# Two-layer retention, Fourier and convolution backbone on one core: stacked retention states, norm roots by column groups, low halves on GpSimd, other orders in the mixers and in the first output stage

## The chip, the cores and the metric

One NeuronCore of a Trainium2 chip runs the whole program. The metric is the device time of one execution in microseconds (us). The engines are named as the profile names them: PE (TensorE matmul), PEld (its weight loads), DVE (VectorE), ACT (ScalarE), POOL (GpSimd), SP (SyncE, which issues most DMAs; SPq is its queue). L1251 is line 1251 of the kernel before.

## The reference

Two layers over a latent stream x (512 tokens of 1024 channels) and a context stream (256 tokens), all float32. Cut to what matters here:

```python
for l in range(2):
    sh1, sc1, g1, sh2, sc2, g2 = split(silu(c) @ w_mod[l] + b_mod[l])          # six modulation vectors, per stream
    h = rmsnorm(x) * (1 + sc1) + sh1                                          # context likewise
    q, k, v, gate, f, cb, cc, ch = split(h @ w_in[l])                         # 3072 columns
    o  = retention(rope(q), rope(k), v) forwards + the same backwards         # 8 heads of 64, chunks of 128 tokens
    o  = o * rsqrt(mean(o * o, per head) + eps) * silu(gate)
    y  = concat(o, real(fft2(f)), cb * dwconv3(cc * ch))
    x  = x + g1 * (y @ w_out[l])
    h  = rmsnorm(x) * (1 + sc2) + sh2
    val, g = split(dwconv3(h @ w_up[l], w_conv))
    x  = x + g2 * ((val * silu(g)) @ w_down[l])
return rmsnorm(x) * final_norm_g
```

Retention of a chunk is the masked scores times the values (intra), plus the queries, scaled by a per-row decay xi, times the state before the chunk (cross). The state of a direction is `S <- decay * S + k^T (zeta * v)`, a 64x64 matrix per head. The latent scans start from the states that the two context chunks leave.

## The kernel before

**Dense products.** Activations lie transposed, channels on partitions. Each weight matrix is cut into "slabs" of 128 output channels by 1024 inputs (512 KB). SP loads them one after the other from HBM (`load_slab`, L328), together with the modulation weights (`load_mods`, L342), which VectorE reduces against the conditioning vectors with a custom dot product (L737) and finishes at L740. GpSimd splits every slab in two halves of four blocks, each into a rounded high part `w_hi` (L446) and a low part `w_lo` (L448), and counts four `split` per slab. TensorE makes one 128x128 block of a slab (a "tile", L1251) from three products in the fast float32 format, hi·hi, lo·hi and hi·lo: six matmuls for both streams in layer 0 (512 latent and 256 context columns), three in layer 1, where the context only feeds kv. Two pairs of PSUM banks alternate between slabs.

**Norms.** The n1_0 norm at the start sums the squares with matmuls whose weights are 128 columns of squares and whose moving operand is a column of ones (L1340), so that one column of results comes for each 128 tokens; ScalarE takes the square roots, VectorE the reciprocals, and TensorE spreads them over the partitions with the identity (L1439). The other norms (n2_0, n1_1, n2_1) come in two parts, one for each stream or half, with sums at L1375 and roots at L1384. For each of eight channel blocks of a part VectorE scales (L877), ScalarE adds the shift and rounds to `h_hi` (L545), VectorE takes the rest `h_lo` (L883), and `part_tile` (L1359) uses both at once.

**The mixer.** After the kv and q slabs, `mixer_plan` (L138) deals the steps of retention evenly among the 96 tiles of the cch, cbf and g slabs (conv, Fourier and gate columns); all engines walk through this one list. A state step is 8 matmuls (L1539) for one direction and one chunk; VectorE makes `vz` (L1037) just before and adds into the state just after (L1047 to L1052). The states of a head pair lie as two 64x64 blocks in a 128x128 block that is zero elsewhere; memsets clear them (L941). A chunk is four steps: scores (L1555), out (cross product of both directions L1569, intra L1575), sums of squares per head (L1583, 4 matmuls with two moving columns) and roots spread per head (L1590, 8 matmuls). On VectorE these are qxi (L1065), the masked scores St (L1069), the reciprocal (L1073) and the product (L1077). Layer 0 has 10 state steps and 6 chunks, layer 1 10 and 4. TensorE waits for all transposed keys (`k_moved`) before the list begins; the last rope (L956 to L958, Y block 3) comes on VectorE at the first chunk's scores. After the list come the channel transforms of the Fourier part (L1606 to L1612) and its sequence products (L1640, L1644), then the out stage.

**Other pieces.** ScalarE makes the decay tables (L475 to L484) and VectorE combines them (`log_decays` L760 to L772, `decays` L779 to L784), in layer 0 right after the first norm and the first kv slab. In the out stage of layer 0 SP brings two slabs and six pairs of mods for the second norm in an order written out by hand. `keep_busy` issues matmuls of no use to anyone while TensorE would wait.

## Time and profile before

| | us |
|---|---|
| median of 3 executions | 1621.41 |
| lowest, highest | 1615.40, 1622.27 |
| the profiled execution's own time | 1619.17 |
| its span in the profile | 1617.4 |
| busy in the span: PE, DVE, POOL, ACT | 1559.5, 919.3, 888.8, 331.7 |
| share of PE and of DVE in the chain that ended last | 64%, 22% |
| HBM read | 165.44 MB, 104 GB/s over the span |
| mean granted clock of TensorE | 0.983 of full speed |

The busy time of an engine is a sum over its instructions. Matmuls overlap in the pipeline, so the time of a group of them is best read from the start of its first to the start of what comes next.

### The profile page before, as it was taken

What the parts mean: (1) busy time and instruction counts of PE and PEld (TensorE: products, weight loads), DVE (VectorE), ACT (ScalarE), POOL (GpSimd) and SP (SyncE); (2) the same over time, 40 slices, a digit from 0 to 9 for tenths busy, and PEclk for the clock granted to TensorE, in tenths of its full rate; (3) what the DMA queues carried; (4) which work ended last, traced back from release to release, by engine and by line L of the source; (5) the groups of instructions that cost most, each with busy time, mean ns of one, the idle gap of its engine ahead of it and who ended that gap; (6) DMA issues with size and microseconds to landing.
All of it is one profiled execution on the core that took longest, in us unless ns stands there. A gap on an engine that the chain in (4) does not pass through costs nothing.

```text
span 1617.4 us, 24334 instructions
## 1 busy us (share of the span) xinstructions
PE 1559.5 (96%) x8962; PEld 1325.4 (82%) x8962; DVE 919.3 (57%) x1367; ACT 331.7 (21%) x512; POOL 888.8 (55%) x830
## 2 busy tenths in 40 slices
PE   7989999999999999999999999999998999999997
PEld 5778888887788888888888888877778888888886
DVE  3876444498887865873378646454545441341444
ACT  3602111311312101120021224111223220220221
POOL 2264333475455565654565544554464776777764
PEclk7999999999999999999999999999999999999999
DMA  8453111244234343332333323231222323233223
GB/s 333 146 168 100 58 40 40 89 154 145 92 130 130 110 142 115 128 130 77 106 125 109 105 80 100 82 92 53 66 78 66 104 93 100 92 99 108 91 91 105
DMA packets 50082, 172.63 MB, mean 107 GB/s; under 512 B 6241, under 2 KB 8801, under 8 KB 48993
## 3 DMA queue, kind: packets, MB, share of 16 engines
q1 hardware_dynamic: 46080, 165.70, 30.6%
q10 hardware_dynamic: 3936, 6.06, 1.3%
q8 instruction: 42, 0.69, 0.2%
q14 instruction: 24, 0.19, 0.0%
HBM read 165.44 MB, written 2.10 MB: 104 GB/s over the span
## 4 chain that ended last, share of the span: by engine, by line
PE 64%; DVE 22%; issue 7%; ACT 3%; DMA 2%; POOL 1%; DVEq 1%; ACTq 1%; SPq 0%
PE pair L1251 51%; DVE aux L737 6%; PE pair L1359 5%; DVE tg L1189 3%; DVE tv L1189 3%; DVE hid_lo L1217 1%; DVE tv L1214 1%; ACT tv L707 1%; ACT hid_hi L715 1%; PE aux L1569 1%; DMA raw<-in_slabs 1%; PE aux L1539 1%; PE aux L1640 1%; DVE h_lo L883 1%; DVE mod_acc L737 1%
## 5 line engine op out<-in xcount | busy, mean ns | idle before, releaser
L446 POOL TENSOR_SCALAR w_hi<-raw 128x512 fp32r<-128x512 f32 (+1 forms) x412 | 298.5, 725 | 674.3 <-PE pair L1251 530.7
L448 POOL TENSOR_TENSOR w_lo<-raw,w_hi 128x512 fp32r<-128x512 f32 (+1 forms) x412 | 592.0, 1437 | 34.4
L1251 PE MATMUL pair<-h_hi,w_hi 128*128 128x512 f32 x1760 | 530.7, 359 | 13.9 <-DVE tv L1189 5.0
L1251 PE MATMUL pair<-h_lo,w_hi 128*128 128x512 f32 x1760 | 523.5, 355 | 1.6 <-DVE h_lo L1091 1.4
L1251 PE MATMUL pair<-h_hi,w_lo 128*128 128x512 f32 x1760 | 521.7, 354 | 0.0
L1251 PEld LDWEIGHTS pair<-h_hi,w_hi 128*128 128x128 f32 x1760 | 288.6, 189 | 66.5 <-issue 13.1
L1251 PEld LDWEIGHTS pair<-h_lo,w_hi 128*128 128x128 f32 x1760 | 288.8, 189 | 51.1 <-DVE h_lo L1091 3.1
L1251 PEld LDWEIGHTS pair<-h_hi,w_lo 128*128 128x128 f32 x1760 | 288.6, 189 | 45.9
L737 DVE CUSTOM_DVE_ANT_0 aux<-mod_slot,c_b 128x1024 f32<-128x1024 f32 x160 | 234.8, 1467 | 4.8 <-DMA mod_slot<-in_mods 2.1
L1144 DVE SCALAR_TENSOR_TENSOR x<-pair,modv,x 128x256 f32 (+3 forms) x84 | 53.0, 658 | 169.0 <-PE pair L1251 168.8
L1251 PE MATMUL pair<-hid_hi,w_hi 128*128 128x512 f32 x486 | 146.8, 356 | 0.2 <-POOL w_lo L448 0.2
L1251 PE MATMUL pair<-hid_lo,w_hi 128*128 128x512 f32 x486 | 146.9, 356 | 0.1
L1251 PE MATMUL pair<-hid_hi,w_lo 128*128 128x512 f32 x486 | 146.7, 356 | 0.0
L1189 DVE SCALAR_TENSOR_TENSOR tg<-pair,vecs,tg 128x511 f32<-128x511 f32 (+1 forms) x132 | 87.0, 659 | 83.2 <-ACT tg L710 75.1
L1189 DVE SCALAR_TENSOR_TENSOR tv<-pair,vecs,tv 128x511 f32<-128x511 f32 (+1 forms) x132 | 87.2, 661 | 81.0 <-ACT tv L707 72.7
L1251 PEld LDWEIGHTS pair<-hid_lo,w_hi 128*128 128x128 f32 x486 | 80.1, 188 | 14.5 <-DVE hid_lo L1217 0.8
L1251 PEld LDWEIGHTS pair<-hid_hi,w_hi 128*128 128x128 f32 x486 | 80.1, 188 | 14.3 <-issue 0.5
L1251 PEld LDWEIGHTS pair<-hid_hi,w_lo 128*128 128x128 f32 x486 | 80.2, 188 | 13.8
L707 ACT ACTIVATE tv<-pair,vecs 128x768 f32<-128x768 f32 (+1 forms) x44 | 35.0, 796 | 260.1 <-PE pair L1251 205.9
L710 ACT ACTIVATE tg<-pair,vecs 128x768 f32<-128x768 f32 (+1 forms) x44 | 35.1, 798 | 178.6 <-PE pair L1251 178.5
L1217 DVE TENSOR_TENSOR hid_lo<-tv,hid_hi 128x768 f32 (+1 forms) x44 | 43.1, 980 | 44.7 <-ACT hid_hi L715 44.7
L713 ACT ACTIVATE tg<-tg 128x768 f32<-128x768 f32 (+1 forms) x44 | 32.6, 741 | 137.4 <-DVE tg L1189 137.4
(177 smaller groups left out, 1329.6 us busy)
## 6 DMA issues: line engine op xcount, KB each, us to landing
raw<-in_slabs SPq DMA_DIRECT2D x206, 512.0 KB, 3.5
mod_slot<-in_mods SPq DMA_DIRECT2D x80, 512.0 KB, 3.5
start_slot<-in_start_mods SPq DMA_DIRECT2D x8, 1024.0 KB, 15.4
x<-in_x SPq DMA_DIRECT2D x4, 768.0 KB, 9.6
rot<-kT ACTq DMA_DIRECT2D x32, 64.0 KB, 2.0
rot<-Y ACTq DMA_DIRECT2D x32, 64.0 KB, 2.1
out<-fin SPq DMA_DIRECT2D x16, 128.0 KB, 1.9
c_b<-in_c SPq DMA_DIRECT2D x1, 512.0 KB, 7.6
```

What stands on the lines that cost most here:

```text
L446: nc.gpsimd.tensor_scalar(w_hi[p][:, a:b], raw[p][:, a:b], 1.0, 1.0, ALU.mult, ALU.mult).then_inc(split, 1)
L448: nc.gpsimd.tensor_tensor(w_lo[p][:, a:b], raw[p][:, a:b], w_hi[p][:, a:b].bitcast(fp32), ALU.subtract).then_inc(split, 1)
L707: nc.scalar.activation(tv[:, 0:nlat], pair[0][:, 0:nlat], ACT.Copy, scale=vec_dyn("ffnw", w))\
L710: nc.scalar.activation(tg[:, 0:nlat], pair[1][:, 0:nlat], ACT.Copy, scale=vec_dyn("ffnw", w + 3 * NHB)).then_inc(s["tg_ready"], 1)
L713: nc.scalar.activation(tg[:, 0:nlat], tg[:, 0:nlat], ACT.Silu).then_inc(s["silu_ready"], 1)
L715: nc.scalar.activation(hid_hi[:, i, 0:nlat], tv[:, 0:nlat], ACT.Copy)\
L737: chain(nc.vector.tensor_tensor_reduce(out=aux01[:, :], in0=slab, in1=c_b[:, st, :], scale=1.0, scalar=0.0, op0=ALU.mult, op1=ALU.add, acc ...
L1144: nc.vector.scalar_tensor_tensor(x[:, 2 * i + p, a0:a1], pair[p][:, a0:a1], modv[:, st, bass.ds(2 * i + (c0 + p), 1)], x[:, 2 * i + p, a0: ...
L1189: ins = nc.vector.scalar_tensor_tensor(dst, src, vec_dyn("ffnw", w + tap), dst, ALU.mult, ALU.add)
L1217: nc.vector.tensor_tensor(hid_lo[:, i, 0:nlat], tv[:, 0:nlat], hid_hi[:, i, 0:nlat].bitcast(fp32), ALU.subtract)\
L1251: ins = nc.tensor.matmul(out[:, a:b], wt, xt[:, a:b], start=first and k == 0, stop=last and k == 2)
L1359: ins = nc.tensor.matmul(pair[p][:, a:b], wt[p][:, w], xt[:, k, a:b], start=opens and j == 0, stop=n == len(order) - 1 and j == 2, skip_gr ...
```

## The change

- (a) Forward and backward states are stacked, forward on partitions 0 to 63 and backward on 64 to 127. A state step does both directions of one pair of chunks with 16 matmuls; there are 5 such steps in a layer. `vz` has two buffers and is made, with the decayed state, one step ahead on VectorE. The cross product of a chunk is 8 matmuls with 64-column weights over both directions at once; qxi is made in four pieces of 64 partitions, two of which go from one half of the partitions to the other. The memsets are gone, and later scores also wait for the chunk before (`o_ready`).
- (b) The plan begins with 8 tiles, gives a state step twice the tiles of another, and the wait for `k_moved` comes at the first state step. The last rope comes before the list.
- (c) Sums of squares and head sums take the ones (or a 32-column pattern) as weights and give 128 columns in groups of 32 rows. Square root and reciprocal then run over 128 columns; roots are spread with 32-row selectors. n1_0 has two of each.
- (d) The channel transforms 0 and 1 go among the last four tiles of the plan.
- (e) In n2_0, n1_1, n2_1 blocks 3 to 7 of part 0 get their low half from GpSimd, before it splits slab 2 of up, kv, up; ScalarE adds the shift in place and then copies. Part 1's pair of slabs runs with a lag of 5 blocks.
- (f) In layer 0 `log_decays` moves to the second kv slab and `decays` to the third; ScalarE waits for them before it moves the values.
- (g) The second half of a narrow slab, which is padding, is no longer split.
- (h) In the first out stage mods go one pair earlier than before against the slabs.
- (i) `keep_busy` has 14 instead of 10, and 2 more before the roots; a constant table is 164 columns wider.

```diff
+MIXER_LEAD = KB
+MIXER_TAIL = 4
+STATE_SHARE = 2
...
-    for c in range(NLC - 1, 0, -1):
-        items.append(("state", 1, c, ("b", c), ("b", c - 1)))
...
+    items = [("state", (c0, None, 4), (c1, None, 4)), ("state", (c1, 4, 0), (c0, 4, 3))]
     if l == 0:
...
+        items += [("chunk", c0, T, slice(HD, P), 4), ("chunk", c1, T + CH, slice(0, HD), 4)]
+    pairs = [("state", (c, c, c + 1), (NLC - 1 - c, NLC - 1 - c, NLC - 2 - c)) for c in range(NLC - 1)]
+    chunk = [("chunk", c, c * CH, slice(0, P), c) for c in range(NLC)]
+    return items + [pairs[0], pairs[1], chunk[1], pairs[2], chunk[2], chunk[0], chunk[3]]
...
+        upto = MIXER_LEAD + spread * sum(shares[:n + 1]) // sum(shares)
         plan += tiles[used:upto] + [step]
...
+    return plan + tiles[used:used + half] + [("channels", 0), ("channels", 1)] + tiles[used + half:]
...
             sp.wait_ge(S[0]["o_ready"], NLC + NCC)
+
+            load_mods(m, MODS_FIRST_OUT[0])
+            m += MODS_FIRST_OUT[0]
             for i in range(KB // 2):
                 for p in range(2):
-                    load_mods(m, MODS_FIRST_OUT[i] // 2)
-                    m += MODS_FIRST_OUT[i] // 2
                     s = PLAN[0, "out"] + 2 + 2 * i + p
                     sp.wait_ge(split, 4 * (s - 1))
                     load_slab(s, p)
+                    if i + 1 < KB // 2:
+                        load_mods(m, MODS_FIRST_OUT[i + 1] // 2)
...
+                if half and narrow(s):
+                    return
...
+            def lows(name):
...
+                for k in range(DVE_LOWS, KB):
+                    pool.wait_ge(norms[name]["hi_ready"], k + 1)
+                    nc.gpsimd.tensor_tensor(h_lo[:, k, a:b], nt[k % 2][:, a:b], h_hi[:, k, a:b].bitcast(fp32), ALU.subtract)\
...
+            behind = {PLAN[0, "up", 0] + 2: "n2_0", PLAN[1, "kv"] + 2: "n1_1", PLAN[1, "up", 0] + 2: "n2_1"}
             for s in range(PLAN["end"]):
+                if s in behind:
+                    lows(behind[s])
...
+                    if j == (0 if l else 2):
                         decays(l)
+                act.wait_ge(s["decay_ready"], 1)
...
+                scaled_values(0)
+                rope(Y[:, HB - 1, 0:T], 2 * HB - 1)
+                dve.wait_ge(s["roped"], 2 * HB)
...
+                            for d, (_, prev, to) in enumerate(item[1:]):
+                                r = slice(HD * d, HD * d + HD)
+                                nc.vector.tensor_tensor(state[r, to, :, :], U[r], state[r, to, :, :], ALU.add)\
                                     .then_inc(s["state_ready"], 1)
-                        dve.wait_ge(s["state_ready"], 2 * n_state)
+                        dve.wait_ge(s["state_ready"], states_ready(n_state))
+                        if n_state < len(pairs):
+                            scaled_values(n_state)
+                            decayed(n_state)
...
-                        for d, st in ((0, fwd), (1, bwd)):
-                            nc.vector.tensor_tensor(qxi[:, d, :, :], q, xi[:, d, :, :], ALU.mult)\
-                                .then_inc(s["qxi_ready"], 1)
+                        for d in range(2):
+                            for hh in range(2):
+                                to, r = slice(HD * d, HD * d + HD), slice(HD * hh, HD * hh + HD)
+                                nc.vector.tensor_tensor(qxi[to, hh, :, :], q[r], xi[r, d, :, :], ALU.mult)\
+                                    .then_inc(s["qxi_ready"], 1)
...
-                        nc.vector.reciprocal(rinv[:, 0:H], rs[:, 0:H]).then_inc(s["hrinv_ready"], 1)
+                        nc.vector.reciprocal(roots[:, 1, :], roots[:, 0, :]).then_inc(s["hrinv_ready"], 1)
...
+                        g = c % 4 * CG
+                        ins = nc.tensor.matmul(aux(2 + c // 4)[g:g + CG, 0:P], ones[:, 0:1].to_broadcast([P, CG]),
+                                               buf[:, c * P:c * P + P], start=part == 0, stop=part == 1)
...
+                for g in range(groups):
+                    ins = nc.tensor.matmul(out[:, g * P:g * P + P], small[r, 8 + g:9 + g].to_broadcast([groups * CG, P]),
+                                           roots[r, part, :], start=True, stop=True)
...
-                for part, lag in ((0, 3), (1, 1)):
+                for part, lag in ((0, 3), (1, 5)):
...
-                    keep_busy(10)
+                    keep_busy(14)
...
-                pe.wait_ge(s["k_moved"], NLC + NCC)
...
+                        for hd in range(H):
+                            for d in range(2):
+                                ins = nc.tensor.matmul(aux(3)[HD * d:HD * d + HD, hd * HD:hd * HD + HD],
+                                                       ktok[:, item[1 + d][0], hd * HD:hd * HD + HD], vz[d][:, hd, :],
+                                                       start=True, stop=True)
...
+                                nc.tensor.matmul(aux(2)[HD * hh:HD * hh + HD, b * CH:b * CH + CH],
+                                                 state[rows, slot, 2 * b + hh, :], qxi[rows, hh, b, :],
+                                                 start=b == 0, stop=True, skip_group_check=b > 0)
...
+                            ins = nc.tensor.matmul(aux(3)[b * CG:b * CG + CG, 0:CH], head_sum, osq[:, b, :],
+                                                   start=True, stop=True)
...
+                            ins = nc.tensor.matmul(aux(b)[:, 0:CH], head_row[g], roots[g, 1, :], start=True, stop=True)
```

## Rows read from the trace of the kernel before

**Rows 1.** Busy time by stretch: start:end, length, PE, PEld, DVE, ACT, POOL, clock, DMA share, GB/s.

```profile
17.00:31.00 14.00, 12.52 (x81) 10.44 (x81) 3.46 (x10) 2.04 (x5) 7.04 (x8) 0.62 0.91 356
97.00:106.00 9.00, 4.55 (x17) 3.95 (x18) 8.83 (x11) 0.54 (x1) 7.86 (x6) 0.81 0.61 203
165.00:309.00 144.00, 141.29 (x1113) 119.81 (x1112) 60.94 (x102) 21.01 (x31) 47.54 (x48) 1.00 0.13 41
309.00:326.00 17.00, 13.37 (x77) 11.60 (x78) 12.15 (x16) 10.72 (x15) 12.23 (x12) 1.00 0.45 165
1070.00:1175.00 105.00, 98.90 (x731) 78.55 (x730) 54.01 (x89) 16.62 (x25) 51.48 (x49) 1.00 0.20 63
```

**Rows 2.** The chain that ended last, in order of time: a run of full tiles.

```profile
560.55 66.83 PE pair L1251 x384
```

**Rows 3.** Timeline of PE, one layer 0 chunk: start, us, instruction, xrecords (two a matmul in retention).

```profile
230.33 1.05 PE L1569 MATMUL aux<-qxi,S_f 128*128 128x128 f32 x8
...
232.21 1.09 PE L1575 MATMUL aux<-St,vtok 128*64 128x128 f32 x16
233.23 0.62 PE L1251 MATMUL pair<-h_hi,w_hi 128*128 128x512 f32 x2
...
235.46 0.95 PE L1583 MATMUL aux<-ident_small,osq 128*128 128x2 f32 x8
236.27 0.59 PE L1251 MATMUL pair<-h_hi,w_hi 128*128 128x512 f32 x2
...
239.56 1.09 PE L1590 MATMUL aux<-ident_small,rinv 128*64 128x128 f32 x16
```

**Rows 4.** Timeline of PE at the start of the program.

```profile
16.76 2.72 PE L1340 MATMUL aux<-ones,sq_sum 128*128 128x1 f32 x12 [2.97 <-DVE sq_sum L792]
...
21.97 1.93 PE L1307 MATMUL aux<-start_slot,c_cols 128*32 128x256 f32 x16
...
43.49 1.07 PE L1307 MATMUL aux<-start_slot,c_cols 128*32 128x256 f32 x16
```

**Rows 5.** Timeline of all engines around the stall in kv.

```profile
60.71 5.42 DVE L769 SCALAR_TENSOR_TENSOR ldt<-ldt 128x48 f32<-128x48 f32 x7
...
93.34 0.43 SPq L328 DMA_DIRECT2D raw<-in_slabs  x1
...
97.89 1.70 POOL L446 TENSOR_SCALAR w_hi<-raw 128x512 fp32r<-128x512 f32 x1 [7.62 <-DMA raw<-in_slabs]
...
101.45 0.63 PE L1251 MATMUL pair<-h_hi,w_hi 128*128 128x512 f32 x2 [4.76 <-POOL w_lo L448]
```

**Rows 6.** The group of the head reciprocals, whole span: xcount, busy us, mean ns, idle before.

```profile
L1073 DVE RECIPROCAL rinv<-rs 128x8 f32<-128x8 f32 x10 | 2.0, 203 | 58.8 <-ACT rs L660 58.8
```

**Rows 7.** Timeline of DVE: the wider reciprocal, two copies in other quarters, two qxi.

```profile
59.06 0.45 DVE L764 RECIPROCAL ldt<-ldt 128x48 f32<-128x48 f32 x1
...
162.86 0.88 DVE L1047 COPY S_b<-aux 64x256 f32<-64x256 f32 x2 [0.79 <-PE aux L1539]
...
1159.04 2.82 DVE L1065 TENSOR_TENSOR qxi<-Y,xi 128x512 f32<-128x512 f32 x2
```

**Rows 8.** The group of qxi, first in the mixer of layer 0, then of layer 1.

```profile
L1065 DVE TENSOR_TENSOR qxi<-Y,xi 128x512 f32<-128x512 f32 x12 | 7.8, 688 | 0.2
...
L1065 DVE TENSOR_TENSOR qxi<-Y,xi 128x512 f32<-128x512 f32 x8 | 7.9, 1032 | 0.1
```

**Rows 9.** Timeline of PE in layer 1's mixer: the first scores.

```profile
1099.16 1.05 PE L1555 MATMUL aux<-Y,kT 64*128 64x128 f32 x14 [2.44 <-DVE Y L958]
```

**Rows 10.** Timeline of SP's queue in the first out stage.

```profile
339.22 8.10 SPq L342 DMA_DIRECT2D mod_slot<-in_mods  x2
```

**Rows 11.** Groups of one norm block's operations and of the slab split, whole span.

```profile
L448 POOL TENSOR_TENSOR w_lo<-raw,w_hi 128x512 fp32r<-128x512 f32 x380 | 555.9, 1463 | 31.7
...
L877 DVE SCALAR_TENSOR_TENSOR nt<-aux,modv,x 128x512 f32<-128x512 f32 x16 | 11.8, 746 | 4.2 <-PE aux L1384 3.9
...
L545 ACT ACTIVATE h_hi<-nt,modv 128x512 fp32r<-128x512 f32 x16 | 11.4, 722 | 11.2 <-DVE nt L877 11.2
```

More of the change, by code:

```diff
@@ L105, in norm_parts, with low_ready @@
     return [(0, 0, T), (1, T, TC)] if name in NORMS[:2] else [(0, 0, C), (0, C, T)]
+DVE_LOWS = 3
+def low_ready(norms, pool_low, name, part, k):
+    if part == 0 and k >= DVE_LOWS:
+        return pool_low, (KB - DVE_LOWS) * NORMS.index(name) + k - DVE_LOWS + 1
+    return norms[name]["h_ready"], (DVE_LOWS if part else 0) + k + 1
 MODS_KVQ = [3, 3, 2, 2, 2, 0]
@@ L149, in mixer_plan @@
              for j in range(n) for k in range(KB)]
-    plan, used = [], 0
+    plan, used = tiles[:MIXER_LEAD], MIXER_LEAD
+    spread, shares = len(tiles) - MIXER_LEAD - MIXER_TAIL, [STATE_SHARE if s[0] == "state" else 1 for s in steps]
     for n, step in enumerate(steps):
-        upto = len(tiles) * (n + 1) // len(steps)
+        upto = MIXER_LEAD + spread * sum(shares[:n + 1]) // sum(shares)
         plan += tiles[used:upto] + [step]
         used = upto
-    return plan
+    half = MIXER_TAIL // 2
+    return plan + tiles[used:used + half] + [("channels", 0), ("channels", 1)] + tiles[used + half:]
 def build_program(nc, io):
@@ L936, in norm_in_parts @@
                     low(1, k)
-            def clear_states():
-                for t in state.values():
-                    chain(nc.vector.memset(t[:, :, :, :], 0.0))
             m = 0
@@ L1373, in part_sums, with spread @@
                     pe.wait_ge(*wait)
-                    for c in range(a // P, b // P):
-                        ins = nc.tensor.matmul(aux(3)[:, c:c + 1], buf[:, c * P:c * P + P], ones[:, 0:1],
-                                               start=part == 0 and i == 0 and c == 0, stop=True, skip_group_check=True)
+                    for g in range((b - a) // P):
+                        ins = nc.tensor.matmul(aux(3)[g * CG:g * CG + CG, part * P:part * P + P],
+                                               ones[:, 0:1].to_broadcast([P, CG]),
+                                               buf[:, a + g * P:a + g * P + P], start=i == 0, stop=i == 1)
                 ins.then_inc(s["sums_done"], 1)
+            def spread(out, part, groups):
+                r = slice(0, groups * CG)
+                for g in range(groups):
+                    ins = nc.tensor.matmul(out[:, g * P:g * P + P], small[r, 8 + g:9 + g].to_broadcast([groups * CG, P]),
+                                           roots[r, part, :], start=True, stop=True)
+                return ins
             def part_roots(name, part):
@@ L1382, in part_roots @@
                 pe.wait_ge(s["rinv_ready"], 2 * NORMS.index(name) + part + 1)
-                for c in range(a // P, b // P):
-                    ins = nc.tensor.matmul(aux(2 + part)[:, c * P - a:c * P - a + P],
-                                           rinv[:, c:c + 1].to_broadcast([P, P]), ident[:, :], start=True, stop=True)
-                ins.then_inc(s["rbc_ready"], 1)
+                spread(aux(2 + part), part, (b - a) // P).then_inc(s["rbc_ready"], 1)
             def slabs_into_norm(first, order, hi, lo, cols, ready, name, free):
@@ L1436, in spread_roots @@
                 s = norms[name]
-                pe.wait_ge(s["rinv_ready"], 1)
-                for c in range(ncol // P):
-                    ins = nc.tensor.matmul(aux23[:, c * P:c * P + P], rinv[:, c:c + 1].to_broadcast([P, P]),
-                                           ident[:, :], start=True, stop=True)
-                    if c in (NLC - 1, NLC + NCC - 1):
-                        ins.then_inc(s["rbc_ready"], 1)
+                for part, n in enumerate((NLC, NCC)):
+                    pe.wait_ge(s["rinv_ready"], part + 1)
+                    spread(aux(2 + part), part, n).then_inc(s["rbc_ready"], 1)
             pe.wait_ge(fills, 2)
@@ L1691, in tables @@
                            np.full(P, T ** -0.5), np.full(P, -T ** -0.5),
-                           np.arange(P) % CG == 0, np.arange(P) % CG == 1], axis=1))
+                           np.arange(P) % CG == 0, np.arange(P) % CG == 1]
+                          + [np.arange(P) == CG * g for g in range(4)], axis=1))
+    row, half = np.arange(P)[:, None], np.arange(P)[None, :] // HD
+    parts.append(row // HD == np.arange(CG)[None, :] // (CG // 2))
+    parts.append((row % CG == half * (CG // 2)))
     return np.concatenate(parts, axis=1).astype(np.float32)
```

293 lines of the change are left out of this document (146 added, 147 removed).

## The prediction

> **What bounds the kernel now.** I read the page's busy shares first: PE is busy 96% of the span. The chain of waits says the same: most of it is full tiles, back to back. A run of it has 64 tiles (384 matmuls) in 66.83 us, 1.04 us each [rows 2]. None of these products changes, so time can only come from what TensorE does beside them, from where it stands still, and from its clock. The table by stretch shows where that is [rows 1]: at the start the granted clock is 0.62, so TensorE works near its 1.2 GHz level; at 97 to 106 us it is busy 4.55 of 9 us; in the mixer of layer 1 it is busy 98.90 of 105 us; in that of layer 0 141.29 of 144 us, so there only work, not waiting, can be saved. VectorE is busy half of the mixers or less. The timeline then prices single steps. A matmul of retention has two records, so x16 is 8 matmuls, and a step's price is the distance from its start to the next start.
>
> **The mixers: TensorE's own work.** In a latent chunk the cross product takes 232.21 - 230.33 = 1.88 us for 16 records of 128 rows of weights by 128 columns; its successor has the shape of L1575, 16 records by 64 rows, which took 233.23 - 232.21 = 1.02 [rows 3]. Eight latent chunks save 0.86 each, 6.9. The head sums take 0.81 for 8 records [rows 3]. Their successor puts 8 records of 32 rows by 128 columns into four row groups. Nearest is L1307 with 32-row groups, 1.07 us for 16 records of 256 columns at full clock [rows 4]: 0.067 each, half of it for 128 columns, so 0.27 plus a fill, 0.31: 0.50 saved, ten chunks, 5.0. The head roots take what L1575 takes, 1.02 for 16 records (1.09 by the record [rows 3]); 8 records in four row groups of the weights I put at 0.40: 0.62 saved, 6.2 for ten. Bounds: groups that don't run side by side cost 0.111 a record (rival below), ideal ones 0.27. A state step has 16 matmuls instead of 8, but half as many steps: equal work, but 10 fewer interruptions of the stream of tiles (and 4 more elsewhere), which I put at 0.2 us each (no row isolates one; bounds 0 and 0.4): 1.3. Sum 19.4.
>
> **The mixers: waits.** Today's waits there are 2.7 of 144 in layer 0, of which I take 2.4, and 6.1 of 105 in layer 1 [rows 1], among them 2.44 for the last rope at the first scores [rows 9]. With the rope done under 8 lead tiles these go, and so does the wait before each Fourier part (PE stands 3.6 of the 17 us there [rows 1], of which I give 1.5 a layer to this wait, bounds 0 and 2), since transforms 0 and 1 are among the last tiles: 11.5 together. In their place comes one long string on VectorE where a chunk stands right behind a state step: 2 adds, 2 vz, 2 decays, 4 qxi, 2 St, twelve operations before the out step. The qxi pieces have 64 partitions but still 512 columns, so I price each as a whole one: 0.69 in layer 0, 1.03 in layer 1 [rows 8]. Layer 0: 12 x 0.69 = 8.2, under it lie 3 tiles, the scores and 2 tiles with their switches, 6.7: 1.6 late, twice. Layer 1: 4 x 1.03, four at about 0.85, four that read PSUM at 0.69: 10.3, under it 7 tiles of 0.68, scores and switches, 6.25: 4.1 late; the next chunk 6.5 against 5.6, 1.0; the others 0.3 twice. New waits 8.9. A stop of 4 us may bring a stretch at the lower clock, as behind the 4.76 us stop in kv; 1.7. Mixers: 19.4 + 11.5 - 8.9 - 1.7 = 20.3.
>
> Two of the qxi pieces change partitions. The two copies of L1047 that do so took 0.88 together at 0.42 each [rows 7], so nothing of one ran under the other, and I count the strings without any overlap. The Trainium skill ("VectorE: DVE Perf Modes", "Two Vector instructions with no wait between them") has it that an instruction whose start quadrant differs starts only when all earlier ones have finished; the pair agrees, and by that rule a string would be some 0.3 us longer, an estimate.
>
> **The start.** The n1_0 sums occupy 21.97 - 16.76 = 5.2 us [rows 4], 24 records each of both buffers at the lower clock. In 32-row groups, at 0.12 a record of 256 columns (1.93 for 16 [rows 4]), half of that for 128, they take 1.45, bounds 0.8 to 1.7. Against it, two square roots and two reciprocals of 128 columns: a reciprocal of 48 columns took 0.45 [rows 7], of 8 columns 0.20 [rows 6], 0.006 a column, so 0.95 for 128; in all 1.3 more. The rest of the start lies behind DMA (0.91 share [rows 1]) and a low clock: if the 6 more matmuls of `keep_busy` hold the clock up from 17 us on, where 0.62 is granted, up to 5 us come on top. I take 5.3, bounds 2 and 10.
>
> **The stall in kv.** Ahead of it VectorE works off log_decays (seven operations of 0.8, 5.42 us [rows 5]) and decays before the mod dots; SP's order is mods, then slabs, and a mod load waits for a used slot. So the slab issued at 93.34 lands at 97.89 after 7.62 us of POOL waiting and TensorE stands 4.76 [rows 5]. With both moved behind kv slabs 1 and 2 the mods are used earlier and SP is not held; the decay work is then covered by the kv and q slabs, and without that cover it would cost its 5.4 and more. I count the 4.76, and 1.9 for the slow clock after it (0.81 in this stretch [rows 1], 19% of 9 us): 6.6, bounds 3 and 8. ScalarE's new wait for `decay_ready` has the moves of the values behind it; nothing reads these before the first state step.
>
> **The norms.** Two sums and two roots in each of three norms save 0.5 to 1 us by the same prices, the wider sqrt and reciprocal take 0.8 each back on the path of part 0. The GpSimd lows: before, a block costs VectorE 0.75 (L877) and about as much for the low half, 1.5; now a block goes round nt, ScalarE twice (0.72 each) and GpSimd (1.46 as for w_lo) [rows 11], with two buffers (0.75 + 2 x 0.72 + 1.46) / 2 = 1.8 a block, against 1.5: five blocks, 1.5 us late in each norm, less what VectorE gains by starting part 1 early. Slab 2's split waits behind these in POOL's queue, which has a slab of lead. I take -0.5 for all three, bounds -8 (each block late) and +6.
>
> **The rest.** Mods one pair earlier in the out stage of layer 0: SP stood there 8.10 us in a mod load with a slab behind it [rows 10], and slabs now stand behind one pair more. VectorE's dots bound that stage; -1, bounds -8 and 0. Padding not split: GpSimd's time is covered by TensorE's tiles, a half's 1.46 for w_lo [rows 11] and the half as long w_hi lie under four tiles of 1.04; what it gives is an earlier next slab at two places, +0.4, bounds 0 and 1. The memsets and `ident_small` lie under other work: 0. If their cover were gone they cost some 5 and 0.1.
>
> **Sum.** 20.3 + 5.3 + 6.6 - 0.5 - 1 + 0.4 = 31.1 us less than the profiled execution's own 1619.17, 1588. It stands 2.2 below the median of 1621.41, so 1590 at the median.
>
> **Rivals.** *More comes back.* The clock stays high over the start (+5), the new waits are mostly covered (+8): a gain of 44, 1577. For it: VectorE has half its time free. Chance 0.13.
>
> *VectorE and GpSimd get in each other's way.* qxi takes 0.69 in layer 0 and 1.03 in layer 1, where GpSimd is busy 51.48 of 105 us [rows 1, 8], and once 2.82 for two [rows 7]. With four pieces in place of two, a string has twice the exposure: 1.5 more in each of ten chunks and three stretches at the lower clock: gain 14, 1607. The Trainium skill ("SBUF — State Buffer", "Who interferes with whom") says that a VectorE instruction with two SBUF inputs and a GpSimd instruction that reads SBUF exclude each other, the later one fully blocked; the two means agree. Against it: the means hold that already. Chance 0.13.
>
> *The change doesn't do what it says.* The 32-row groups don't run side by side: a record 0.111 with all its fill, 0.89 for the sums and the roots each, so 11 of the mixers' gain and 3 of the start's are gone: gain 17, 1604. For it: no row shows four different row groups of weights. Chance 0.08.
>
> *Slower.* The two qxi pieces that change partitions cost double or more, and stand before the out step: 3.3 more in each of ten chunks, 33, with 17 for the clock that falls at each stop: 1637. It decides if a piece takes over 1.3 to 1.7 us. Against it: the shifted copies of L1047 took 0.42 for 256 columns [rows 7], which is half a whole piece of 0.69 and some fixed time. Chance 0.04.
>
> **Range and chances.** My forecast has 0.62. To hold 8 in 10 the range takes it with its bounds and the nearer edges of the first three rivals: 1577 to 1606. What a measurement can tell here from no change is about 0.5%, 8.1 us. Faster by more: 0.92, since the three rivals but the last lie there; within 0.5%: 0.04, where the norms' and the out stage's worst bounds join a rival; slower: 0.04.
>
> **What would show it.** In the profile after: the start's sums near 1.5 us; no 4.76 us stop near 100 us; cross product 1.02, head sums 0.31, head roots 0.40; a wait of PE for qxi or St of 1.6 us twice in layer 0 and of 4 us once in layer 1, with a lower clock after it; qxi pieces of 0.69 and 1.03; part 0 of the norms no more than 2 us longer. Wrong would be: pieces over 1.3 us, waits of PE for `rot` or for POOL's lows, or a stop in out.

## The result, and the profile after

The changed kernel takes 1606.7 us (median of 8 executions, 1604.39 to 1611.71) against 1620.82 (8 executions, 1612.36 to 1623.31): a ratio of 0.9926, 95% interval 0.991 to 0.9943. It is faster, by 14 us; I had forecast 31 us and 1590, with a range that ended at 1606. The profiled execution took 1607.85 us (1619.17 before), its span is 1606.1 us.

The page of the kernel after: busy times, and the chain by engine.

```profile
PE 1547.5 (96%) x8910; PEld 1296.8 (81%) x8910; DVE 933.3 (58%) x1331; ACT 340.9 (21%) x529; POOL 900.5 (56%) x841
...
PE 84%; DVE 9%; DMA 2%; POOL 2%; ACT 1%; issue 1%; SPq 0%; ACTq 0%; DVEq 0%; POOLq 0%
```

TensorE is what it was, 96% busy. Both traces hold 7386 matmuls of dense products, in the same order but for a few tiles of the norms, so the start of the n-th of them is a mark at which the two traces can be laid side by side. I worked this table out from the two traces:

```
matmul   stage that ends there           before    after    gain so far   forecast of the stage
     0   (first product)                   30.9     26.5        4.4
   600   start and kv of layer 0          164.9    150.6       14.3           11.9
  1176   mixer 0, Fourier                 331.6    312.8       18.7       ) 20.3 with
  1344   out stage 0                      360.7    347.0       13.6       ) mixer 1; -1
  1656   rest of out, norm n2_0           431.2    415.5       15.7       ) -0.5 for three norms
  4656   up and down of layer 0           954.5    946.4        8.1            0
  5100   norm n1_1, kv of layer 1        1041.8   1032.7        9.1
  5550   mixer 1                         1205.8   1192.5       13.3
  last   rest of layer 1                 1607.1   1595.4       11.7
```

The last mark has 11.7 us of gain where 31.1 were forecast. The missing 19.4 us are mainly in three places: the mixers brought 8.6 instead of 20.3, the out stage lost 5.1 instead of 1, and the up and down stages of layer 0, which the change does not touch and which I had at nothing, lost 7.6. The stages behind mixer 1 lost 1.6 more. Against that the start, kv and the norms ahead of mixer 1 brought 6 more than forecast.

**The mixers: the steps are as short as forecast, the waits are not.** Timeline of PE after: the second chunk of layer 0, which is a context chunk (one direction, 64 partitions), and then a latent chunk, which is the one to be laid beside [rows 3]. In the context chunk what follows these four rows starts at 195.90, 196.92, 200.65 and 203.37 us.

```profile
194.88 1.09 PE L1662 MATMUL aux<-qxi,state 64*64 64x128 f32 x16
195.90 1.09 PE L1668 MATMUL aux<-St,vtok 128*64 128x128 f32 x16
...
200.30 0.42 PE L1677 MATMUL aux<-osq,ident_small 128*32 128x128 f32 x8
...
202.94 0.50 PE L1685 MATMUL aux<-roots,ident_small 32*128 32x128 f32 x8
...
251.67 1.09 PE L1662 MATMUL aux<-qxi,state 128*64 128x128 f32 x16 [0.40 <-DVE St L1134]
252.57 1.07 PE L1668 MATMUL aux<-St,vtok 128*64 128x128 f32 x16
```

The cross product of a latent chunk takes 252.57 - 251.67 = 0.90 us, where 1.02 was forecast and 1.88 was the time before. (1.02 is what the context chunk takes, 0.98 before.) The head sums take 0.35 and the head roots 0.43; 0.31 and 0.40 were forecast. So the 32-row groups do run side by side, and the rival of the 0.111 us record falls. The same view at the first chunk shows where the gain goes, and the table of PE's waits sums it up (us in total, times, longest).

```profile
171.16 0.62 PE L1316 MATMUL pair<-h_hi,w_hi 128*128 128x512 f32 x2
...
176.48 1.82 PE L1662 MATMUL aux<-qxi,state 64*64 64x128 f32 x16 [2.92 <-DVE St L1134]
178.23 1.97 PE L1668 MATMUL aux<-St,vtok 128*64 128x128 f32 x16
```

```profile
PE aux L1662 <- DVE St L1134: 17.2, 7, 6.2
...
PE pair L1316 <- POOL w_lo L477: 1.9, 1, 1.9
```

TensorE waits 17.2 us for the masked scores, and after this wait the out step (cross product and intra) takes 3.65 us, where it took 2.04 in the second chunk above: the clock has fallen (0.96 of full speed on average in that mixer, 0.97 in the other). Of the seven waits the three longest, of 2.9, 4.6 and 6.2 us, have a stretch at the lower clock at their end; those of 0.4 to 1.7 us have none.

```profile
150.00:292.00 142.00, 134.11 (x1087) 110.68 (x1087) 74.09 (x97) 21.65 (x31) 48.09 (x46) 0.96 0.14 46
...
1055.00:1162.00 107.00, 97.69 (x735) 76.17 (x733) 67.18 (x83) 19.74 (x31) 53.64 (x50) 0.97 0.20 63
```

The timelines of VectorE and of GpSimd at this place, and VectorE's with the window narrowed to single pieces:

```profile
166.81 1.41 DVE L1113 TENSOR_TENSOR state<-aux,state 64x512 f32<-64x512 f32 x2 [1.09 <-PE aux L1626]
168.25 1.29 DVE L1069 TENSOR_TENSOR vz<-vtok,zeta 128x512 f32<-128x512 f32 x2
169.47 1.40 DVE L1077 TENSOR_TENSOR state<-state,cdec 64x512 f32<-64x512 f32 x2
170.90 4.11 DVE L1130 TENSOR_TENSOR qxi<-Y,xi 64x512 f32<-64x512 f32 x4
175.04 1.29 DVE L1134 TENSOR_TENSOR St<-aux,mask 128x512 f32<-128x512 f32 x2
...
170.31 1.04 POOL L475 TENSOR_SCALAR w_hi<-raw 128x512 fp32r<-128x512 f32 x1 [3.62 <-PE pair L1316]
171.43 1.61 POOL L477 TENSOR_TENSOR w_lo<-raw,w_hi 128x512 fp32r<-128x512 f32 x1
...
171.91 1.67 DVE L1130 TENSOR_TENSOR qxi<-Y,xi 64x512 f32<-64x512 f32 x1
...
173.61 0.68 DVE L1130 TENSOR_TENSOR qxi<-Y,xi 64x512 f32<-64x512 f32 x1
```

That is the string of twelve. A piece of qxi takes 0.68 us when GpSimd is idle, 0.98 when `w_lo` starts during it, and 1.67 when it starts while `w_lo` runs; and so through the whole trace: of 40 pieces 22 take 0.67 to 0.69 us, the 18 others 0.98 to 1.67, and each of the 18 overlaps a `w_lo` for 0.45 us or more. A `w_hi` alone did not lengthen a piece: the one at 189.54 us overlaps one for 0.65 us and takes 0.69. It is not the shift between partitions either: all four kinds of piece come with 0.69 us or less where GpSimd is idle. One `w_lo` that meets the string costs it 1.3 us, and every fourth tile brings one. The Trainium skill ("SBUF — State Buffer", "Who interferes with whom") has the two engines contend when VectorE reads two SBUF operands and GpSimd reads SBUF. For `w_lo` the trace agrees, with 0.68 against 1.67 us; beside a `w_hi`, which reads SBUF too, it is mostly the `w_hi` that is longer (up to 1.13 us, 0.62 alone). The masked scores and the adds to the states, which read one operand from PSUM, take 0.67 to 0.70 us beside GpSimd as well.

The string can be summed from its rows. In layer 0 the first runs from 166.81 to the end of St at 176.33, 9.5 us where 8.2 was forecast: 1.3 more, and the wait is 2.9 instead of 1.6. The second meets two `w_lo` and takes 11.0, 2.8 more, and the wait is 4.6. The first string of layer 1, from VectorE's timeline:

```profile
1085.37 2.78 DVE L1077 TENSOR_TENSOR state<-state,cdec 64x512 f32<-64x512 f32 x2
...
1088.79 1.40 DVE L1113 TENSOR_TENSOR state<-aux,state 64x512 f32<-64x512 f32 x2
...
1097.90 1.29 DVE L1134 TENSOR_TENSOR St<-aux,mask 128x512 f32<-128x512 f32 x2
```

It takes 1099.19 - 1088.79 = 10.4 us, and 10.3 was forecast. But it starts 2.0 us late: TensorE's state step ended at 1086.81, and VectorE was still at the decayed states that it makes a step ahead. With the 4.1 us forecast that gives the wait of 6.15.

**The out stage.** SP's queue after, in the first out stage, then GpSimd and PE there:

```profile
322.33 6.12 SPq L365 DMA_DIRECT2D mod_slot<-in_mods  x2
328.50 0.43 SPq L351 DMA_DIRECT2D raw<-in_slabs  x1
...
333.19 1.68 POOL L475 TENSOR_SCALAR w_hi<-raw 128x512 fp32r<-128x512 f32 x1 [7.77 <-DMA raw<-in_slabs]
...
336.92 0.87 PE L1316 MATMUL pair<-h_hi,w_hi 128*128 128x512 f32 x2 [1.93 <-POOL w_lo L477]
```

The slab that SP issues at 328.50 stood behind a pair of mods for 6.12 us, as I had named it; PE then waits 1.93 us for its low part and falls to the lower clock (0.86 over 333 to 345 us). The fall belongs to this one execution. From mark 1200 to mark 1350 the kernel before takes 26.0 us, this profile 30.2, but the second profile of the same kernel (run 2) 27.8, with a wait of 1.4 us and the clock at 1.00:

```profile
333.00:345.00 12.00, 10.64 (x60) 8.98 (x60) 11.83 (x17) 0.85 (x1) 9.45 (x7) 1.00 0.46 171
```

The profiles of runs 3, 5, 7, 8 and 9, which keep SP's new order, have 27.8 to 28.0 us there and a clock of 1.00. So the order costs about 1.8 us; the other 2.4 us come from the clock in this execution.

**Up and down of layer 0.** A full tile is three pairs of matmuls; the timeline of PE before and after at 650 us, both in an up stage at a granted clock of 1.00:

```profile
649.73 0.51 PE L1251 MATMUL pair<-h_lo,w_hi 128*128 128x512 f32 x2
...
650.77 0.51 PE L1251 MATMUL pair<-h_lo,w_hi 128*128 128x512 f32 x2
```

```profile
650.01 0.53 PE L1316 MATMUL pair<-h_lo,w_hi 128*128 128x512 f32 x2
...
651.07 0.53 PE L1316 MATMUL pair<-h_lo,w_hi 128*128 128x512 f32 x2
```

From one h_lo to the next it is 650.77 - 649.73 = 1.04 us before and 651.07 - 650.01 = 1.06 after. Nothing waits; the same instructions go by in another rhythm, tile after tile. Over the 500 tiles between marks 1656 and 4656 the rhythm makes the 7.6 us. Of these, 2.2 us are in the first up group (marks 1656 to 2304).

### The profile page after: what moved, and what is told of

Read it like the earlier page. It is cut to its first block, busy times and chain, and to the rows that moved or that the text cites. A ratio compares the mean times of both kernels' runs of the same rounds, so it can differ in the third digit from the quotient of the medians.

```text
span 1606.1 us, 24230 instructions
## 1 busy us (share of the span) xinstructions
PE 1547.5 (96%) x8910; PEld 1296.8 (81%) x8910; DVE 933.3 (58%) x1331; ACT 340.9 (21%) x529; POOL 900.5 (56%) x841
## 4 chain that ended last, share of the span: by engine, by line
PE 84%; DVE 9%; DMA 2%; POOL 2%; ACT 1%; issue 1%; SPq 0%; ACTq 0%; DVEq 0%; POOLq 0%
PE pair L1316 76%; PE pair L1425 3%; DVE qxi L1130 2%; DVE h_lo L939 1%; DVE nt L933 1%; DMA start_slot<-in_start_mods 1%; POOL w_lo L477 1%; PE aux L1662 1%; DMA raw<-in_slabs 1%; PE aux L1668 1%; PE aux L1578 1%; PE aux L1626 1%; DVE St L1134 1%; DVE aux L790 1%; POOL w_hi L475 1%
## 5 line engine op out<-in xcount | busy, mean ns | idle before, releaser
L477 POOL TENSOR_TENSOR w_lo<-raw,w_hi 128x512 fp32r<-128x512 f32 (+1 forms) x410 | 585.5, 1428 | 34.3
L790 DVE CUSTOM_DVE_ANT_0 aux<-mod_slot,c_b 128x1024 f32<-128x1024 f32 x160 | 223.9, 1399 | 4.3 <-DMA mod_slot<-in_mods 1.1
L1316 PEld LDWEIGHTS pair<-hid_lo,w_hi 128*128 128x128 f32 x486 | 80.6, 188 | 13.6
L1282 DVE TENSOR_TENSOR hid_lo<-tv,hid_hi 128x768 f32 (+1 forms) x44 | 47.1, 1070 | 44.7 <-ACT hid_hi L768 44.7
L1425 PE MATMUL pair<-h_lo,w_hi 128*128 128x256 f32 (+1 forms) x160 | 53.6, 335 | 7.8 <-DVE h_lo L939 6.1
## 6 DMA issues: line engine op xcount, KB each, us to landing
start_slot<-in_start_mods SPq DMA_DIRECT2D x8, 1024.0 KB, 15.6
```

The source lines that it names most:

```text
L477: nc.gpsimd.tensor_tensor(w_lo[p][:, a:b], raw[p][:, a:b], w_hi[p][:, a:b].bitcast(fp32), ALU.subtract).then_inc(split, 3 if narrow(s) else 1)
L790: chain(nc.vector.tensor_tensor_reduce(out=aux01[:, :], in0=slab, in1=c_b[:, st, :], scale=1.0, scalar=0.0, op0=ALU.mult, op1=ALU.add, acc ...
L1282: nc.vector.tensor_tensor(hid_lo[:, i, 0:nlat], tv[:, 0:nlat], hid_hi[:, i, 0:nlat].bitcast(fp32), ALU.subtract)\
L1316: ins = nc.tensor.matmul(out[:, a:b], wt, xt[:, a:b], start=first and k == 0, stop=last and k == 2)
L1425: ins = nc.tensor.matmul(pair[p][:, a:b], wt[p][:, w], xt[:, k, a:b], start=opens and j == 0, stop=n == len(order) - 1 and j == 2, skip_gr ...
```

## The experiments

Twelve runs were made, each beside the kernel before; ratios are to that, with 95% intervals. A granted clock at the start of the program that differs from one execution to the next moves single profiles by 2 to 4 us (0.67 over 31 to 47 us in the profiles of runs 3 and 4, 1.00 in those of the changed kernel and of run 2), so the marks are compared from stage to stage.

### Runs 1 and 2: both kernels once more

> The kernel before, once more. In the profiled pair, a full tile of six matmuls in the up and down stages of layer 0 took 1.040 us before and 1.060 (up) or 1.053 (down) after, through nearly all of 425 to 950 us, and between 50 and 75 us it was 1.060 in both. Theory 1, the pitch is a property of the program: this run shows 1.040 again between 425 and 950 us. Theory 2, it is a property of the single execution: this run may show 1.053 to 1.060 over long stretches, and is then some 8 to 13 us longer than a run without.

> The changed kernel, once more. Theory 1 (property of the program): 1.060 and 1.053 us a tile over 425 to 950 us again, time near 1607. Theory 2 (property of the execution): some stretches at 1.040, time lower by 0.02 us for each such tile, down to about 1597. Both: TensorE waits before the out steps of a chunk (St, VectorE) come to 17 us again, with two of over 3 us in layer 0.

Run 1 took 1620.69 us, run 2 1605.39. Run 1: tiles at 1.060 from 430 to 545 us, the first up group, and 1.040 from there to 950. Run 2: 1.060 and 1.053 from 415 to 940, as in the first profile. The rhythm of the first up group comes and goes, that of all the later stages is the program's; theory 1 holds from 545 us on. Against run 1, which has the slower first group as well, the changed kernel loses 5.2 us between marks 1656 and 4656, not 7.6. In run 2 St was waited for as in the first profile (17.3 us in all, the longest 6.2).

### Run 3: vz and decayed states behind the chunk

```diff
                         if n_state < len(pairs):
-                            scaled_values(n_state)
-                            decayed(n_state)
+                            if queue[queue.index(item) + 1][0] == "scores":
+                                held.append(n_state)
+                            else:
+                                scaled_values(n_state)
+                                decayed(n_state)
                         continue
...
+                        for n in held:
+                            scaled_values(n)
+                            decayed(n)
+                        held = []
```

> Changed kernel, but where a chunk stands right behind a state step, the two vz and the two decayed states for the next state step are made after the chunk's masked scores instead of before its qxi: four operations of 0.69 to 1.3 us less in that string. Theory A (the string on VectorE, lengthened by GpSimd, sets the waits before the out steps): of the 17 us of waits for St at most 5 are left, the lower clock behind them goes too, 9 to 14 us faster than the changed kernel (about 0.993 of it, 0.984 of the kernel before). Rival (the waits come from the scores or from the states, not from the string): unchanged within 2 us.

1593.1 us, ratio 0.9841 (0.9815 to 0.9867), 13.6 us below the changed kernel. PE's waits in run 3:

```profile
PE aux L1670 <- DVE St L1138: 6.5, 6, 2.7
```

17.2 us have become 6.5; the marks gain 10.6 us over mixer 0 and 5.0 over mixer 1 (10.0 and 4.0 if run 2 is the one to compare with), more than the 10.7 us of waits, since the stretches at the lower clock go with them (1.00 over the whole of mixer 0, 147 to 300 us). Theory A asked for at most 5 us of waits, and 6.5 are left; its time was met. The string on VectorE set the waits. VectorE's string at the first chunk, now with one qxi piece lengthened and no wait of PE behind it:

```profile
169.30 1.41 DVE L1114 TENSOR_TENSOR state<-aux,state 64x512 f32<-64x512 f32 x2 [1.09 <-PE aux L1634]
170.75 3.20 DVE L1134 TENSOR_TENSOR qxi<-Y,xi 64x512 f32<-64x512 f32 x4
173.98 1.29 DVE L1138 TENSOR_TENSOR St<-aux,mask 128x512 f32<-128x512 f32 x2
```

### Run 9: and qxi ahead of the state step

```diff
+                        nxt = queue[queue.index(item) + 1]
+                        if nxt[0] == "scores":
+                            scaled_queries(nxt[2])
+                            early = True
                         dve.wait_ge(s["u_done"], n_state)
```

> The kernel of run 3 (vz and decayed states behind the masked scores), and besides the four qxi pieces made ahead of the wait for the state step in front of the chunk, where VectorE stood idle. The string between that state step and the out step is then two adds and two St. Theory A (length of the string on VectorE): of run 3's 6.5 us of waits for St at most 2 are left; 3 to 5 us faster than run 3, near 1589. Rival (what is left in run 3 is in layer 1 and comes from GpSimd's blocking or from chunks that stand behind no state step): 1592 to 1594, waits for St above 4 us.

1588.95 us, ratio 0.981 (0.9786 to 0.9833): the time is what theory A gave, but 4.1 us of waits are left, not 2; one of them takes 2.6:

```profile
PE aux L1682 <- DVE St L1150: 4.1, 3, 2.6
```

All three are in layer 1, the longest at its first chunk. VectorE was not idle there, as the expectation had it: from 1070.12 us on it works through vz, the decayed states, z and the four qxi pieces without a break, and comes to the two adds late.

```profile
1072.44 2.78 DVE L1077 TENSOR_TENSOR state<-state,cdec 64x512 f32<-64x512 f32 x2
...
1075.86 4.10 DVE L1091 TENSOR_TENSOR qxi<-Y,xi 64x512 f32<-64x512 f32 x4
1079.99 1.41 DVE L1128 TENSOR_TENSOR state<-aux,state 64x512 f32<-64x512 f32 x2
```

### Run 4: SP's old order in the first out stage

```diff
-            load_mods(m, MODS_FIRST_OUT[0])
-            m += MODS_FIRST_OUT[0]
             for i in range(KB // 2):
                 for p in range(2):
+                    load_mods(m, MODS_FIRST_OUT[i] // 2)
+                    m += MODS_FIRST_OUT[i] // 2
...
-                    if i + 1 < KB // 2:
-                        load_mods(m, MODS_FIRST_OUT[i + 1] // 2)
-                        m += MODS_FIRST_OUT[i + 1] // 2
```

> Changed kernel with the kernel before's order in SP's queue in the first out stage: a pair of mods before each slab instead of one pair ahead. In the changed kernel's profile TensorE waits 1.9 us for a slab's split there, the clock falls, and 4.1 us of the gain are lost against the kernel before from 345 to 360 us of the latter. Theory A (the slab stands behind a mod load that waits for VectorE): no wait for w_lo there, 3 to 4 us faster than the changed kernel. Rival (VectorE's dot products bound the stage, whichever order): the wait moves to mods, drained or Fourier's end, within 1 us of the changed kernel, or slower by up to 3.

In the profile there is no wait for w_lo in the out stage, as theory A has it, and the clock is at 1.00 over 333 to 350 us. Between marks 1200 and 1350 it takes 26.5 us: 3.7 less than the first profile of the changed kernel, of which 0.9 goes again in the norm behind, but only 1.3 less than run 2. So SP's order is worth about 1.3 us, and theory A's 3 to 4 us came from a profile with a stretch at the lower clock. In the time it can't be told: 1607.79 us, ratio 0.9925 (0.9896 to 0.9955) with four executions from 1604.26 to 1610.94; the profiled one is the longest of them.

### Runs 5 and 6: 32 bytes

```diff
-    work = top[0]
+    work = top[0] + 32
```

> Changed kernel with 32 bytes of gap ahead of the work area, in which the hidden units, Y, the scratch of norms and mixer lie. The change had moved that area by 1632 bytes, so 32 bytes off the alignment to 64 of the kernel before; here it is 1664, the old alignment. All four profiles of changed kernels so far show full tiles of layer 0 at 1.060 (up) and 1.053 (down) us from 425 to 950 us, both of the kernel before 1.040 from 540 us on. Theory P (the place of the hidden units in SBUF sets the pitch of the down tiles, and the stream keeps that rhythm into the up tiles): 1.040 over 540 to 950 us, 7 to 9 us faster than the changed kernel (near 1598). Rival (instruction order, GpSimd's new work or chance): 1.053 and 1.060 again, time unchanged within 2 us.

> Kernel before with the same 32 bytes of gap, which take its work area off the alignment to 64. Theory P: tiles at 1.053 and 1.060 us over 540 to 950 us, 7 to 9 us slower than the kernel before (ratio 1.005). Rival: 1.040 there, ratio 1.000.

Timeline of PE at 560 us, in the first down stage, first the changed kernel, then run 5:

```profile
560.15 0.52 PE L1316 MATMUL pair<-hid_lo,w_hi 128*128 128x512 f32 x2
...
561.20 0.52 PE L1316 MATMUL pair<-hid_lo,w_hi 128*128 128x512 f32 x2
```

```profile
560.08 0.51 PE L1316 MATMUL pair<-hid_lo,w_hi 128*128 128x512 f32 x2
...
561.12 0.51 PE L1316 MATMUL pair<-hid_lo,w_hi 128*128 128x512 f32 x2
```

561.12 - 560.08 = 1.04 in run 5, 1.05 in the changed kernel; in run 6 the down tiles of the kernel before go at 1.060. So the place of the work area, in which the hidden units lie, sets the rhythm of the down tiles, both ways. The up tiles did not follow: 1.060 from 600 us on in run 5, 1.040 in run 6. That half of theory P fell. The times, 1604.75 (0.9921, 0.9892 to 0.9949) and 1618.89 (0.9996, 0.9978 to 1.0013), can't show the 2 us of the down tiles.

### Run 7: all low halves on VectorE

```diff
-DVE_LOWS = 3
+DVE_LOWS = KB
```

> Changed kernel with all low halves of the three norms on VectorE again (DVE_LOWS = 8); the lag of 5 stays. My forecast gave the GpSimd lows and their neighbours -0.5 us with bounds -8 and +6. Theory A (they are of little worth): within 2 us of the changed kernel. Rival (they carry the norms' 1 to 2 us each of gain): 2 to 5 us slower than it. If GpSimd's lows set the pitch of the tiles: 1.040 over 540 to 950 us, 7 us or more faster.

1603.84 us, ratio 0.9918 (0.9892 to 0.9945), not to be told from the changed kernel's. By the marks norm n1_1 is 0.7 us shorter, the others the same. GpSimd's lows bring nothing that can be seen here. The later up and down tiles stay at 1.060 and 1.053.

### Run 8: the decays back in their place

```diff
                     norm("n1_0", TC, 0, SC1, SH1)
+                    log_decays()
...
-                    if j == (0 if l else 2):
+                    if j == 0:
                         decays(l)
```

> Changed kernel with log_decays and decays of layer 0 back behind the first norm and the first kv slab. Theory A (VectorE's decay work ahead of the mod dots holds SP's queue and with it a slab): TensorE stands about 4.8 us for a slab near 95 to 100 us again, with a lower clock behind it; 5 to 7 us slower than the changed kernel. Rival (the stall went for another reason, as the earlier start): no stop over 1 us there, within 1.5 us.

1612.4 us, ratio 0.9961 (0.9948 to 0.9975), 5.7 us slower than the changed kernel; the marks lose 5.9 us between 150 and 300. The stop is there again, shorter than in [rows 5], with the clock behind it (0.88 over 92 to 106 us):

```profile
94.44 1.00 PE L1314 MATMUL pair<-h_hi,w_hi 128*128 128x512 f32 x2 [3.90 <-POOL w_lo L477]
```

### Runs 10 and 11: what gained, together, and the lag

Run 10 has the edits of runs 3, 9, 7, 5 and 4. Run 11 has besides:

```diff
-                for part, lag in ((0, 3), (1, 5)):
+                for part, lag in ((0, 3), (1, 1)):
```

> All that gained by itself, together: runs 3 and 9, all low halves on VectorE (run 7), the work area at the old alignment (run 5), SP's old order in the first out stage (run 4). If the parts add up: run 9 less 2 us (run 5, down tiles at 1.040) less 2.5 (run 7) less 0 to 3 (run 4): 1582 to 1587. If run 4 and run 7 gained at the same place (the mark behind the out stage): 1585 to 1588.

> Run 10 with the second part's pair of slabs at a lag of 1 block again, so that the norms stand as in the kernel before but for the roots by column groups. Theory L (the lag's order starts the up tiles in the slower rhythm): up tiles of layer 0 at 1.040 over 600 to 900 us, 5 us faster than run 10. Rival (the rhythm of the up tiles comes from elsewhere): 1.060 as in run 10; then the lag is worth what TensorE waits for h_lo in the second parts, 1 to 3 us slower than run 10.

Run 10: 1582.36 us, ratio 0.9774 (0.9749 to 0.9799), inside the 1582 to 1587 that the parts give when they are added. Run 11: 1587.39, ratio 0.9797 (0.9776 to 0.9819). The intervals overlap. By the marks run 11 loses 2.1 us in norm n2_0 and 1.7 in norm n2_1, and gets 2.2 back in the first up group, which it runs at 1.040; its profile waits longer for tv than run 10's (5.0 us over two waits against 2.2). Theory L fell: the up tiles stay at 1.060 from 600 us on.

### Run 12: the work area at its exact old address

The kernel is run 10's but for this:

```diff
-    ldt = new("ldt", [P, 3, DEPTH * 24])
-    zeta = new("zeta", [P, 2, H])
...
-    roots = new("roots", [P, 2, CH])
...
     work = top[0] + 32
+    top[0] = work + 92160
+    ldt = new("ldt", [P, 3, DEPTH * 24])
+    zeta = new("zeta", [P, 2, H])
+    roots = new("roots", [P, 2, CH])
```

> Run 10, but with the work area at exactly the address of the kernel before instead of 1664 bytes further: the decay logarithms, zeta and the roots lie behind it. In runs 5 and 10 the down tiles were back at 1.040 us, but the up tiles of layer 0 behind them (600 to 700, 775 to 875 us) stayed at 1.060; in all three profiles with the work area at or 32 bytes behind the old address they were at 1.040. Theory P2 (the exact place of the hidden units, beyond the alignment to 64, sets in which rhythm the stream enters the up tiles): 1.040 over 600 to 900 us, 4 to 5 us faster than run 10, near 1578. Rival (something else in the program, as the order or number of instructions): 1.060 over 600 to 700 us, 1581 to 1584.

Timeline of PE at 650 us, first run 10, then run 12:

```profile
649.90 0.51 PE L1333 MATMUL pair<-h_lo,w_hi 128*128 128x512 f32 x2
650.25 0.53 PE L1333 MATMUL pair<-h_hi,w_hi 128*128 128x512 f32 x2
...
650.96 0.51 PE L1333 MATMUL pair<-h_lo,w_hi 128*128 128x512 f32 x2
```

```profile
649.66 0.51 PE L1334 MATMUL pair<-h_lo,w_hi 128*128 128x512 f32 x2
650.01 0.51 PE L1334 MATMUL pair<-h_hi,w_hi 128*128 128x512 f32 x2
...
650.70 0.51 PE L1334 MATMUL pair<-h_lo,w_hi 128*128 128x512 f32 x2
```

1.06 against 1.04 us: with the work area where it had been, the up tiles have their old rhythm, though none of their own operands lies in it. Between marks 2700 and 4500 run 12 is 3.8 us shorter than run 10. 1579.83 us (1576.75 to 1581.89), ratio 0.977 (0.9745 to 0.9795): 37 us less than the kernel before beside it (1617.27). That run 12 is faster than run 10 is read from the marks of one profile each; the two ratios can't be told apart.

## Why the prediction was wrong

**What held.** TensorE's own work in the chunks (0.90, 0.35 and 0.43 us against 1.02, 0.31 and 0.40). The start: the sums took 18.61 - 17.26 = 1.35 us against 1.45 forecast, and with kv it brought 14.3 us against 11.9. That the sums came so close is in part luck: their price was read at the lower clock, they ran at a clock of 1.00, and 0.28 of the 1.35 us was a wait for a DMA. The stall in kv: 6.6 us forecast, 5.9 by the marks of run 8. The norms: 3.1 us over n2_0 and n1_1 with kv of layer 1, where I had -0.5 for all three norms, inside its bounds. That the changed kernel is faster.

**What failed first: the price of the string on VectorE.** I wrote "new waits 8.9" and 1.7 for the clock. I had the right places and the right operations, and priced layer 0 at "0.69 in layer 0", the mean of a stretch in which no `w_lo` met the two-piece qxi; the longer string can't keep out of its way. The four pieces took 4.11 us, not 2.8. In layer 1 the price of 10.3 for the string held, and what failed is that it starts when the state step ends: it started 2.0 us late. St was waited for 17.2 us, the longest 6.2 where I had 4.1, and each of the three longest waits brought its own stretch at the lower clock, of which I had counted one. Run 3 shows the price of the four operations moved out of the string, 10.6 us in mixer 0 and 5.0 in mixer 1; 4.9 of these 15.6 us are beyond the waits and went with the lower clock, where I had 1.7. The 8.3 us of waits and the 3.2 us of clock that I had too little are nearly the 11.7 us that the mixers fell short. That GpSimd lengthens the pieces is read from their overlaps in the trace; no run took GpSimd out of the way. The mechanism is that of the rival of the two engines in each other's way, whose gain of 14 us is what was measured. But that its number matches is luck: the rival had 1.5 us in each of ten chunks and three stretches at the lower clock, while the waits came behind state steps, and the causes below make up the rest of the number.

**Second: a term that was not in the sum.** "None of these products changes, so time can only come from what TensorE does beside them": the products did not change, their pace did. A table that grows and new buffers moved the work area by 1632 bytes, and full tiles of layer 0 went from 1.040 to 1.053 and 1.060 us, 7.6 us over the up and down stages in the profiled pair and 5.2 against run 1. Run 5 gets 2.1 us of it back and run 12 another 3.8 by the place of buffers alone, and run 6 slows the down tiles of the kernel before by it; the 2.2 us of the first up group are not the program's. Part of it could have been read before: the kernel before had 1.06 us tiles for some time at 50 to 75 us and 1.04 later, so two paces of the same instructions were in the trace.

**Third, and smaller: the out stage.** I gave SP's new order -1 with a bound of -8. In the first profile it cost 4.1 us at its place, but 2.4 of these are a stretch at the lower clock that no other profile with this order has; without it the order costs about 1.8 us. VectorE's dots did not bound that stage alone: the slab behind a pair of mods came late, and PE waited. The 1.6 us lost behind mixer 1 are in both profiles of the changed kernel (402.9 and 403.0 us against 401.3 in both of the kernel before), and their cause stays open.

Three sums of the prediction are slightly off, and nothing hangs on them: 19% of 9 us is 1.7 and not 1.9, ten fewer interruptions and four more, six in all at 0.2 us, give 1.2 and not 1.3, and the slower rival's 50 us off the forecast give 1640 and not 1637.

The range ended 0.7 us short of the result: it held each rival by itself, and the waits, dearer than forecast, came together with a loss of 5 us or more that it did not name.

## What to carry to other kernels

A string of operations on a side engine that stands between two steps of the bounding engine is to be priced with its collisions, and what is not needed in it (the next step's operands) belongs behind it: four operations moved were worth 13.6 us. It is also to be asked whether the side engine is free when the string may start. When buffers are added, place them behind the ones that the matmuls read, or compare the pace of unchanged matmuls in the two traces first. Where a wait is followed by a lower granted clock, count both; but look at a second profile of the same kernel before a stretch at the lower clock is put down to the change.

## What the runs showed of the hardware

The same stream of matmuls at a granted clock of 1.00 has several steady rhythms: 1.040, 1.053 and 1.060 us for six matmuls. For the down tiles the rhythm depended on the place of the work area, in which their moving operand lies: 1.040 at the old place and 1664 bytes further on, 1.053 at 1632, 1.060 at 32 bytes. The second and third up group, whose operands had not moved, went at 1.040 in the four profiles with the work area at the old place or 32 bytes further on, and at 1.060 in the ten with 1632 or 1664. It is not simply the pace of the down tiles in front of them that is carried on: those went at 1.040 in runs 10 and 12 alike, and at 1.060 in run 6, where the up tiles went at 1.040. Why these addresses matter, and why the first up group goes at either pace in different executions of one kernel, was not found. Behind mixer 1, with three matmuls a tile, the place of the work area changed the time by 1 us or less.
